# Decoder step on one core: a block of tile 1 moved behind tile 0, three query blocks as token strips, first heads' parts and a GELU moved up

## What is computed

```python
def post_norm_block(x, mix, w_out, ln1_g, ln1_b, peer_w_query, peer_sub_keys, peer_u, peer_v, ln2_g, ln2_b):
    h = layer_norm(ALPHA * x + mix @ w_out, ln1_g, ln1_b)
    return layer_norm(ALPHA * h + peer_ffn(h, peer_w_query, peer_sub_keys, peer_u, peer_v), ln2_g, ln2_b)

def block(xc):                                   # of peer_ffn, PEER_HEADS = 8, K = 16
    q = (xc @ w_query).reshape(PEER_TBLOCK, PEER_HEADS, 2, PEER_QDIM // 2)
    s = jnp.einsum('thcd,ckd->thck', q, sub_keys)
    top_s, top_i = lax.top_k(s, K)
    cand_s = (top_s[:, :, 0, :, None] + top_s[:, :, 1, None, :]).reshape(PEER_TBLOCK, PEER_HEADS, K * K)
    best_s, best_j = lax.top_k(cand_s, K)
    experts, gate = ..., jax.nn.softmax(best_s, axis=-1)
    act = jax.nn.gelu(jnp.einsum('thkd,td->thk', u_tab[experts], xc))
    return jnp.einsum('thk,thkd->td', (gate * act), v_tab[experts])
```

## Time and profile before

| | us |
|---|---|
| median of 3 runs | 2551.88 (2546.99 to 2552.63) |
| profiled execution, its own time | 2548.59 |
| its span in the profile | 2546.7 |
| PE, DVE, POOL, ACT busy | 1781.2, 1274.8, 819.3, 343.6 |
| DMA, mean over the span | 379 GB/s of 965.86 MB |

### The profile page before, as it was taken

One profiled execution on the slowest core, in us unless ns is written; L12 is line 12 of the kernel. 1 busy time (PEld: TensorE's weight loads), 2 busy tenths in 40 slices (PEclk: granted clock), 3 DMA queues, 4 the chain that ended last, 5 costly groups with the idle time before them and its releaser, 6 DMA issues.

```text
span 2546.7 us, 29967 instructions
## 1 busy us (share of the span) xinstructions
PE 1781.2 (70%) x9870; PEld 992.5 (39%) x9870; DVE 1274.8 (50%) x2425; ACT 343.6 (13%) x789; POOL 819.3 (32%) x595
## 2 busy tenths in 40 slices
PE   8999999979999887777855665769533333333335
PEld 5777766544498665555512212217300000000000
DVE  0510122254367867577967343225699544454560
ACT  0000111332131100210101011002110001021111
POOL 0000000000012343332334222323244777767662
PEclk9999999999989888898876777888755555555556
DMA  9789979897469999999999999999999999999998
GB/s 398 301 343 358 369 278 373 341 383 285 163 276 369 379 406 407 408 407 406 369 379 407 399 368 405 413 421 421 407 421 392 422 422 421 421 421 422 422 422 345
DMA packets 213915, 965.86 MB, mean 379 GB/s; under 512 B 23969, under 2 KB 89506, under 8 KB 122850
## 3 DMA queue, kind: packets, MB, share of 16 engines
q0 software_dynamic: 84432, 626.26, 59.9%
q1 hardware_dynamic: 93378, 302.69, 30.8%
q10 hardware_dynamic: 35952, 35.01, 4.1%
HBM read 957.38 MB, written 14.88 MB: 382 GB/s over the span
## 4 chain that ended last, share of the span: by engine, by line
DMA 43%; PE 38%; DVE 11%; issue 4%; ACTq 3%; ACT 1%; POOL 1%; SPq 1%; POOLq 0%; DVEq 0%
DMA sb<-in_peer_v,sb 23%; PE bank L1068 14%; DMA sb<-in_nsa_t 7%; DMA sb<-in_peer_u,sb 7%; DVE sb L2370 4%; PE bank L1420 4%; PE bank L1463 3%; PE bank L1716 3%; PE bank L1376 3%; PE bank L1132 2%; PE bank L1172 2%; DMA sb<-in_nsa_v 2%; DMA sb<-in_w_out 2%; ACTq L441 1%; PE bank L1583 1%
## 5 line engine op out<-in xcount | busy, mean ns | idle before, releaser
L1716 PE MATMUL bank<-sb 128*32 128x512 f32 x2304 | 475.1, 876 | 557.9 <-DMA sb<-in_peer_v,sb 528.5
L2480 POOL DMA_INDIRECT sb<-in_peer_v,sb x288 | 490.4, 1703 | 533.9 <-PE bank L1716 464.0
L2370 DVE CUSTOM_DVE_ANT_1 sb<-sb 128x2048 f32<-128x2048 f32 x192 | 439.6, 2293 | 316.2 <-DMA sb<-in_peer_u,sb 313.0
L2480 POOL DMA_INDIRECT sb<-in_peer_u,sb x288 | 320.5, 1113 | 561.5 <-DVE sb L2370 323.4
L1716 PEld LDWEIGHTS bank<-sb 128*32 128x32 f32 x2304 | 60.7, 127 | 878.1 <-DMA sb<-in_peer_v,sb 809.4
L1068 PE MATMUL bank<-sb 128*128 128x288 f32 x1408 | 350.7, 409 | 12.4 <-DMA sb<-in_w_in 12.4
L1463 PE MATMUL bank<-sb 128*128 128x256 f32 x1024 | 273.2, 426 | 53.7 <-DMA sb<-in_nsa_t 44.5
L1068 PEld LDWEIGHTS bank<-sb 128*128 128x128 f32 x1408 | 266.3, 191 | 95.7 <-DMA sb<-in_tokens_t 12.4
L2370 DVE CUSTOM_DVE_ANT_0 sb<-sb 128x2048 f32<-128x2048 f32 x96 | 219.8, 2292 | 151.9 <-DMA sb<-in_peer_u,sb 150.3
L1463 PEld LDWEIGHTS bank<-sb 128*128 128x128 f32 x1024 | 246.7, 309 | 90.8 <-DMA sb<-in_nsa_t 56.6
L1034 ACT ACTIVATE sb<-sb 128x32 f32<-128x32 f32 x288 | 86.7, 316 | 830.3 <-PE bank L1716 515.2
(11 more groups left out here) (362 smaller groups left out, 1496.5 us busy)
## 6 DMA issues: line engine op xcount, KB each, us to landing
sb<-in_a_k SPq DMA_DIRECT2D x128, 512.0 KB, 6.8
sb<-in_a_v SPq DMA_DIRECT2D x128, 512.0 KB, 6.6
sb<-in_w_in SPq DMA_DIRECT2D x44, 1024.0 KB, 9.2
sb<-in_w_out SPq DMA_DIRECT2D x32, 1024.0 KB, 8.9
sb<-in_w_query SPq DMA_DIRECT2D x32, 1024.0 KB, 9.6
sb<-in_nsa_t SPq DMA_DIRECT2D x200, 128.0 KB, 8.1
sb<-in_nsa_t ACTq DMA_DIRECT2D x184, 128.0 KB, 11.7
sb<-in_nsa_v SPq DMA_DIRECT2D x64, 128.0 KB, 19.9
```

The source lines that it names most:

```text
L1716: mm = pe.matmul(bank[g % 2][32 * c:32 * c + 32, :], diag[j % 4], rows[:, 512 * c:512 * c + 512], start=(s in FIRST), stop=(s in LAST), sk ...
L2370: dve.tensor_tensor_reduce(out=u, in0=u, in1=replica(g), scale=1.0, scalar=0.0, op0=ALU.mult, op1=ALU.add, accum_out=act16[:, r % 2, j:j + ...
L2480: pool.indirect_dma_start(rows[j % 4], None, dram[table], bass.IndirectOffsetOnAxis(ap=idx, axis=0)).then_inc(full[j % 4], 16)
```

## The change

What it does, part by part.

1. Output projection: for n = 2 and n = 3 all of tile 0 goes first (items 8 to 11, then 12 to 15), and tile 1's items 8 to 15 follow in one run. DVE takes tile 0's third and fourth block on two counts of `wo_first`, and tile 1's third block after tile 0's norm.
2. Queries: block 1 goes to bank 5 and block 2 to bank 1. Both first scores of tile 0 now stand ahead of query block 2. Tile 1's blocks 0, 1 and 2 are made with the tokens stationary and the weights moving (`query_parts`), 16 matmuls of 128 columns a block in four strips of bank 4; ACT copies the parts to `q_part` in one piece, `query_sum` adds the strips with three small matmuls against `fold`, ACT copies the sums to `q_one`. Their scores come after block 4.
3. ACT: replicas of the tokens for group 0 (`replicate`, 1.9 us each) are spread between the other pieces, the first ahead of tile 1's square. The replica moves from AT_PROJ + 4096 to AT_H + 4096, where `vcmp` stands later, so the first `cmp_out` of the values' side waits for `u_used` of 64.
4. Selection: head 1's parts move from slots 1, 3, 4 to 0, 1, 2, its experts from slot 5 to 3; heads 2 and 3 from 6 to 11 to 4 to 9, their experts from 12 and 13 to 10 and 11.
5. ACT: `gelu_exp16` stands ahead of the background in its step.

```diff
-        h_rep0, h_rep1 = words(AT_PROJ + 4096, KT, P), words(AT_PROJ + 2048, KT, P)
+        h_rep0, h_rep1 = words(AT_H + 4096, KT, P), words(AT_PROJ + 2048, KT, P)
...
-        HEAD_PARTS = {1: (0, 1, 0), 3: (0, 1, 1), 4: (0, 1, 2)}
-        HEAD_PARTS.update({6 + 3 * k + part: (0, 2 + k, part) for k in range(2) for part in range(3)})
+        HEAD_PARTS = {part: (0, 1, part) for part in range(3)}
+        HEAD_PARTS.update({4 + 3 * k + part: (0, 2 + k, part) for k in range(2) for part in range(3)})
...
-        EXPERT_PARTS = {12: (0, 1, 0), 13: (0, 1, 1), 27: (0, 2, 0), 28: (0, 2, 1), 43: (0, 3, 0), 44: (0, 3, 1)}
+        EXPERT_PARTS = {10: (0, 1, 0), 11: (0, 1, 1), 27: (0, 2, 0), 28: (0, 2, 1), 43: (0, 3, 0), 44: (0, 3, 1)}
...
-        EXPERT_HEADS = {5: (0, 1), QUERY_AT + 6: (2, 0), QUERY_AT + 10: (2, 1)}
+        EXPERT_HEADS = {3: (0, 1), QUERY_AT + 6: (2, 0), QUERY_AT + 10: (2, 1)}
...
             def cmp_out(kv, b):
                 act.wait_ge(cmp_mm, NB * kv + b + 1)
+                if kv and b == 0:
+                    act.wait_ge(u_used, 64)
...
-                background(t)
                 if 17 <= t <= SLOTS_ALL + 1 and t % 16 == 1:
                     gelu_exp16(t // 16 - 1)
+                background(t)
...
-            for k in range(12):
-                if k % 4 == 0 and k >= 8:
-                    pe.wait_ge(wo_evac, 2)
+            for k in range(8):
                 out_rows(k, 0)
                 out_rows(k, 1).then_inc(item_used, 1)
-            pe.wait_ge(wo_evac, 4)
-            for k in range(12, 16):
-                mm = out_rows(k, 0)
-            mm.then_inc(wo_first, 1)
-            for k in range(12, 16):
+            for n in range(2, 4):
+                pe.wait_ge(wo_evac, 2 * n - 2)
+                for k in range(4 * n, 4 * n + 4):
+                    mm = out_rows(k, 0)
+                mm.then_inc(wo_first, 1)
+            for k in range(8, 16):
                 out_rows(k, 1).then_inc(item_used, 1)
...
+            def query_parts(m):
+                w = arrived("wq", m)
+                for kt in range(KT):
+                    own = slice(ROWS_1 * (kt % 4), ROWS_1 * (kt % 4) + ROWS_1)
+                    mm = pe.matmul(bank[4][own, P * m:P * m + P], h_t[:, kt, P:TOK_1], w[:, P * kt:P * kt + P],
+                                   start=(kt < 4), stop=(kt >= KT - 4), skip_group_check=True)
+                mm.then_inc(item_used, 1)
...
-            query_rows(0, 0, P).then_inc(wq_first, 1)
-            query_rows(1, 0, P).then_inc(wq_first, 1)
-            pe.wait_ge(q_in, 1)
-            score_rows(0, 0).then_inc(s_mm, 1)
-            query_rows(2, 0, P)
-            pe.wait_ge(q_in, 2)
-            score_rows(1, 0).then_inc(s_mm, 1)
+            query_rows(0, P).then_inc(wq_first, 1)
+            query_rows(1, P).then_inc(wq_first, 1)
+            for m in range(2):
+                pe.wait_ge(q_in, m + 1)
+                score_rows(m, 0).then_inc(s_mm, 1)
+            pe.wait_ge(wo_evac, 7)
+            query_rows(2, P).then_inc(wq_first, 1)
             turn_prompt(1)
             pe.wait_ge(h_t_in, 8)
-            query_rows(0, P, TOK_1).then_inc(item_used, 1)
-            query_rows(1, P, TOK_1).then_inc(item_used, 1)
+            pe.wait_ge(wo_evac, 8)
+            for m in range(3):
+                query_parts(m)
...
```

More of the change, by code:

```diff
@@ L1443, in _ @@
+            for m in range(5, 16):
+                pe.wait_ge(q_in, m + 1)
+                query_rows(m, TOK_1).then_inc(item_used, 1)
                 score(m - 1)
```

116 lines of the change are left out of this document (74 added, 42 removed).

## The result

The changed kernel took 2527.59 us (median of 6 runs, 2524.48 to 2532.85) against 2552.18 us (6 runs, 2546.31 to 2555.18) for the kernel before: ratio 0.991, 95% interval 0.9895 to 0.9924. A second series, further down, gave 2531.75 against 2548.8 us, 0.9939 (0.9923 to 0.9955). The means of the two, 2529.7 and 2550.5, are 21 us apart; 12 were forecast. The profiled execution took 2527.81 us (span 2525.7).

A forecast was written before the change was run, and what follows sets the result against it. The prediction took DMA idle time once the queries have begun as the bound. 12 (idle time) + 2.5 (heads' parts, GELU) - 2.5 (step 61) = 12 us gained, giving 2540 us from a median of 2551.88; range 2532 to 2550.

The forecast's parts named there:

- What bounds the kernel.: All after the queries is paid in bytes; what counts is DMA engines' idle time, about 24.5 us at the main pause.
- cushion for ACT's copies: New strip-sum copies on ACT: PE may wait 4 us, taken as nothing because block 3 starts at about 708, not 729.30.
- DVE's wait of 8.53 us: DVE's wait for head 1's scores was to vanish, block 3 being done 17 us earlier.
- The first term, 12 us of idle DMA time: Around the first query weights and first gather, idle DMA time falls from 24.5 us by 12.4: 12 us gained.
- the pause itself: PE's idling before tile 0's turning shrinks from 5.36 to 1.3 us, keeping its clock up: 1.5 us gained.
- the bound of 3.7 us: Tile 1's strips, if run one after another, take 3.7 us a block instead of 0.93; 2.8 us of gain go.
- factor of up to 4: Skill's gain for swap and strips: tile 1's first block takes 1.5 us; the forecast stayed with 0.93.
- PSUM Bottleneck: Skill's warning that copies from PSUM become the bound: ACT's 4 us would count, making the sum 8; forecast said not.
- Heads' parts and GELU, 2.5 us: Waits of 9.32 us (POOL, heads 2 and 3) and 10.96 us (DVE, exponential) go: 2.5 us gained, bounds 0 to 6.8.
- Step 61, -2.5 us: ACT's new wait at the ninth `cmp_out` holds it 18.3 us; cost between nothing and 18.3, taken as 2.5 us.
- DVE is the bound in the slots up to 15: Rival: only the first gather's 5.4 us come through, less or more step 61's wait; 2544 to 2549, chance 0.17.
- More comes back: Rival: dips at 740 to 850 us go altogether and step 61 is covered; 19 us, 2533, chance 0.15.

The follow-up runs named there:

- output block alone: Kernel before with only tile 1's third output block moved behind tile 0's last, plus one more PE wait: 2543.67 us, ratio 0.998.
- strips undone: Changed kernel with tile 1's query blocks 0 to 2 made with weights stationary again, in the new place, without sums over strips: 2544.38 us, 0.9978.
- output block undone: Changed kernel with the third output block back ahead of tile 0's last, in PE's and DVE's order: 2535.86 us, 0.9946.
- strips alone: Kernel before with strips and the new order of first query blocks, plus the replica's new buffer and its step 61 wait: 2535.43 us, 0.9948.
- gathers held: Changed kernel with POOL's first gather held until PE has used wq 5, no work added: 2536.04 us, 0.9949.
- four weights ahead: Changed kernel with wq 4 to 7 loaded early into the gathers' empty ring slots; first four gathers wait for their use: 2529.86 us, 0.9926.
- tables undone: Changed kernel with the tables of heads' and experts' parts at their old slots: 2529.97 us, 0.9917.
- two weights ahead: Changed kernel with wq 4 and 5 loaded ahead of wq 0 into idle buffers of the later stage, no gather held: 2531.86 us, 0.9942.
- blocks 8 to 12 shortened: Changed kernel with query blocks 8 to 12 reduced to the first half of their sums, transfers and waits kept: 2532.32 us, 0.9927.
- shortened, two weights ahead: Changed kernel with query blocks 8 to 12 cut to half sums and wq 4 and 5 loaded early into idle buffers: 2528.96 us, 0.9912.
- both late: Changed kernel with query blocks 7 to 11 computed twice and POOL's first gather held until wq 5 is used: 2550.03 us, 1.0007.

## Why the prediction fell short

**What bounds the kernel.** This step failed: "all that follows the queries is paid in bytes", and what counts is "how long the DMA engines stand still". What the runs showed in its place is the lead of PE's chain of query blocks: the first tap comes 21 to 24 us earlier, and the time follows it. I read the DMA share, and not the chain of waits, which in the kernel before stands on PE from the first query block to the first tap (start, us, what):

```profile
694.63 9.00 PE bank L1420 x64
...
709.43 11.85 PE bank L1420 x64
...
721.84 6.97 PE bank L1420 x32
...
791.96 4.54 PE bank L1420 x32
796.51 1.33 PE bank L1408 x8
798.48 7.49 PE bank L1463 x32
```

From there the taps alternate with their page loads, and the rest follows at a distance of 1742 to 1754 us. First tap and end of the span of all 19 traces, in us from T0:

| kernel | first gather | first tap | end | from tap to end |
|---|---|---|---|---|
| before | 108.1 | 186.8 | 1935.0 | 1748.2 |
| blocks 7 to 11 twice, gathers held | 112.8 | 186.6 | 1934.2 | 1747.6 |
| blocks 7 to 11 twice | 101.1 | 186.6 | 1930.5 | 1743.9 |
| exponential alone | 106.5 | 185.2 | 1930.5 | 1745.3 |
| new wait alone | 106.4 | 185.2 | 1930.8 | 1745.6 |
| output block alone | 103.2 | 182.0 | 1924.1 | 1742.1 |
| strips undone | 100.9 | 181.2 | 1927.1 | 1745.9 |
| blocks 8 to 10 twice | 100.9 | 175.2 | 1918.9 | 1743.6 |
| output block undone | 106.6 | 171.3 | 1920.3 | 1748.9 |
| strips alone | 105.3 | 167.9 | 1916.6 | 1748.6 |
| gathers held | 112.6 | 166.1 | 1920.3 | 1754.2 |
| four weights ahead | 107.6 | 166.0 | 1916.7 | 1750.7 |
| the change again | 100.9 | 164.5 | 1913.3 | 1748.7 |
| tables undone | 100.9 | 163.4 | 1913.3 | 1749.9 |
| exponential undone | 100.9 | 163.3 | 1913.4 | 1750.1 |
| two weights ahead | 100.9 | 163.0 | 1913.4 | 1750.3 |
| blocks 8 to 12 shortened | 100.9 | 163.0 | 1914.9 | 1752.0 |
| the change | 100.9 | 162.6 | 1910.9 | 1748.3 |
| shortened, two weights ahead | 101.2 | 161.6 | 1914.9 | 1753.3 |

The distance is a little longer where the tap is early. A straight line through the first taps and the medians of all 19 gives, as an estimate, 0.8 us of time for each us of the tap.

The prediction had the lead in hand: "block 3 starts at about 708 instead of 729.30". It used those 21 us as a cushion for ACT's copies, and priced what the lead itself is worth at DVE's wait of 8.53 us, within the bytes ("since block 3 is done 17 us earlier", where its own figures, near 712.7 against 735.3 us, make it 22.6). The lead at the tap was 24.2 us between the two traces, and 20.7 to 22.6 against the two kernels that run at the time of before; the two series gained 24.6 and 17.1 us. The rows for pricing it were at hand: PE is busy without a pause from block 3 to the tap.

**The first term, 12 us of idle DMA time.** As a size it came out. Of the engines' idle time between T0 and T0 + 160 us (by the share, in stretches of 5 us), 61.2 us before, 45.9 are left; the two kernels that run at the time of before (exponential alone, wait alone) have 57.9 and 58.4, so 12 to 15 went. As a cause it did not. With blocks 7 to 11 doubled 49.3 us are left, so 9 to 12 us of idle time are gone there too, the first gather is as early as in the change, and nothing is gained. T0 + 60 to T0 + 120 us and T0 + 120 to T0 + 200 us, of the kernel before, the change, and the change with these blocks doubled:

```profile
671.67:731.67 60.00, 53.42 (x296) 43.19 (x295) 27.65 (x71) 19.35 (x28) 4.77 (x5) 0.75 0.39 157
731.67:811.67 80.00, 79.34 (x526) 74.77 (x525) 66.57 (x165) 19.60 (x49) 20.16 (x16) 1.00 0.96 380
```

```profile
674.83:734.83 60.00, 56.47 (x495) 45.56 (x493) 39.12 (x107) 26.96 (x43) 5.72 (x6) 1.00 0.62 249
734.83:814.83 80.00, 69.47 (x401) 64.17 (x402) 70.19 (x168) 12.82 (x36) 26.98 (x21) 0.93 0.98 386
```

```profile
676.24:736.24 60.00, 56.45 (x476) 45.78 (x475) 37.73 (x103) 26.81 (x42) 5.73 (x6) 0.94 0.58 235
736.24:816.24 80.00, 79.34 (x533) 76.05 (x532) 59.15 (x141) 12.24 (x35) 17.42 (x15) 1.00 0.88 333
```

The last row also shows what the doubled blocks do not settle: with PE late, the loads behind it come late too (333 GB/s against 386), so late blocks and late bytes go together there. What speaks against the bytes as the cause is the kernel with two weights ahead: it moved 2.2 MB into idle time, of which at least 1.0 MB were handed back by T0 + 160 us, and gained nothing. So the hole was a sign of the late blocks and not the cause of the time. Even as a count, the share was a poor measure: at 740 to 765 us before it reads 0.95, a lack of 5%, while 371 GB/s against 420 after is a lack of 12%.

**Single steps.** Turning starts 4.8 us earlier (4.1 forecast), behind 1.92 us of idling; blocks 0 and 1 took 7.38 us (7.5), but 9.0 to 9.8 in six other traces with this order of work (last section). The forecast had the pause itself at 1.3 us. The three strips took 2.83 us, 0.94 a block (0.93 from the earlier trace rows), so the bound of 3.7 us falls. These blocks took 18.9 us before, 6.7 times as long, part of it at the lower clock; the last of them took 7.04 us at a granted clock of 0.50 throughout (last section). Halved for the upper level that is 3.5 us, an estimate, 3.7 times 0.94. So the Trainium skill's factor of up to 4 (TensorEngine Tiling (Array Packing), When to Use Tiling) agrees with the trace at one clock level; its 1.5 us fall because the forecast applied it to 5.9 us that were partly at the lower level. wq 0 was used 12.3 us earlier (9.9), the first gather came 7.1 earlier (5.4). The same page's PSUM Bottleneck warns that the copies may become the bound, for which the forecast had 4 us; the trace disagrees here, PE waited 0.37 us ahead of the strips, and from there on its timeline shows no wait in any of the blocks.

**Heads' parts and GELU, 2.5 us.** Not shown by any run: alone the exponential is 1.0 (0.999 to 1.001), undone both lie within what two series of one kernel differ by (4.2 us). The wait of 9.32 us went by the tables: it stands at 9.33 us wherever they are as before (tables undone, strips alone, exponential alone), and costs nothing clear. The wait of 10.96 us goes by either way, with the exponential moved alone and with strips alone. That such a wait is long does not tell that it is paid for.

**Step 61, -2.5 us.** The wait was predicted at 18.3 us and is 19.41; its cost is 0 (wait alone: 0.999 to 1.0009). Probably work already handed to PE, DVE and the gathers covers it; no run tests that.

**The rivals.** "DVE is the bound in the slots up to 15" is not borne out: before the change PE's chain was the bound, as the doubled blocks show, and after it PE, once its blocks are shorter, waits for weights and ahead of the tap, not for DVE. What the held gathers cost (4.3 to 8.4 us) is the one hint of it. "More comes back", 2533 us, is nearest in time, for a wrong reason: its dips did fill, but by PE's lead, and the waits that it named are worth nothing by themselves.

**What stays open.** From T0, the first trace of the change is 16.0 us ahead of before at the dot of slot 30 and 24.0 at slot 132; the 8 us between are in no term. Over all 19 traces slots 30 to 132 take 713 to 721 us without order by kernel, and these two traces are the two ends (712.9 and 721.0; the change again has 715.7). So I take it for spread between executions, which the runs do not settle. Open too is how the held gathers come to the longest distance from tap to end, 1754 us, where both late have 1748 and the two shortened kernels, with early gathers, 1752 and 1753; and what PE waits for ahead of the tap in the shortened kernels.

## What to carry to other kernels

Before idle time of a transfer engine is priced, follow the chain of waits through the stretch: an engine that is busy without a pause from the change to the next stage's first instruction passes on every microsecond up to there, and here about 0.8 of each to the end, whatever the DMA share says. A lead that the working finds and uses only as cover is to be priced itself. And after a gain, test the chain in both directions: doubling some of its blocks showed that it had been the bound, halving some that it alone was one no longer.
